# First modulation of a 14-stage kernel: shift and scale loaded before the gate, and x with its norm worked out beside the additions

## The chip, the cores and the metric

The kernel runs on one core of a Trainium2 chip. The metric is device time in microseconds (us) of one execution. Engines are called as in the profile: PE (TensorE, matrix products), DVE (VectorE), ACT (ScalarE), POOL (GpSimd) and SP (SyncE, which here only issues transfers). They run on their own instruction lists and meet at semaphores. SBUF is the on-chip memory of 128 partitions, PSUM the accumulation memory that PE writes.

## The reference, cut to what matters

Two networks follow each other (six sublayers, then eight). Each sublayer takes a 256 x 1024 activation `x`, normalizes it, scales and shifts it by vectors that come from a conditioning vector `c`, applies weights, and adds the result to `x` through a gate. The opening of the first sublayer is what this case is about:

```
c_act = silu(c)
mod = (c_act @ mod_w[layer] + mod_b[layer]).reshape(B, N_SUB, 3, D_MODEL)   # shift, scale, gate of each sublayer
h = rmsnorm(x, g) * (1 + scale) + shift
x = x + 0.5 * (1 + gate) * swiglu(h, w_gu, w_down)
```

`mod_w` has 3 x 1024 columns for each sublayer: 12.6 MB in float32 for the first sublayer. `lru_lambda` (used in the fifth stage) and the rotary positions (used from the seventh stage on) need small elementwise work that is also done in the opening. All arithmetic must stay in float32 quality.

## The kernel before, in words

Everything that streams from memory is float32. Weights come in chunks of 1 MB (`raw`, 4 buffers, issued by SP in `chunk`). A chunk is split in two pieces; ACT copies a piece to a high half (`w_hi`, function `pieces` in the ACT block), DVE subtracts to get the low half (`w_lo`, `pieces` in the DVE block), and PE multiplies three times (`a_hi*w_hi`, `a_lo*w_hi`, `a_hi*w_lo`). There are 4 buffers of pieces (`OPS`). A chunk's transfer waits until the low halves of the chunk four before it are made.

The modulation vectors of a sublayer are called a group. For a group, 16 units of 128 x 1536 of `mod_w` are loaded (`mod_raw`, two buffers, `h` = 0 or 1, issued by POOL in `mod_half`), and DVE adds each, times one entry of `silu(c)` per partition, to `mod_acc` (`mod_add`). PE then sums `mod_acc` over the partitions with 24 one-column products (`mod_sum`), and DVE finishes (`mod_finish`). Groups 1 to 13 are worked through during the stages before they are needed: in a "ffn1" stage one unit is added between every two pieces. POOL loads the next unit into a buffer when DVE has added the one before it (`mod_half` waits for `mod_used`). POOL also makes the low halves of the hidden activations (`hid_low`), one after each job.

A stage of kind "ffn1" starts with eleven jobs of 96 products each; a job needs four pieces. After a job ACT applies silu (`sig`), DVE multiplies (`product`, which frees the job's PSUM banks), ACT writes `hid_hi` and POOL `hid_lo`. A product waits until the low halves of two jobs before are made. In a job's DVE part the order is: two pieces, a unit with h = 0, two pieces, a unit with h = 1, the product. ACT makes the next-but-one job's first piece only behind `hid_hi` of a job.

Group 0 has nothing before it to hide behind. In the opening, SP issues the positions, `x`, 29 small vectors (all into `rows`), then 16 units of `first_mod` (7 buffers), then the weights. PE waits for all small vectors, transposes `x` and `rows`, DVE copies both out of PSUM, ACT makes silu(c) and two steps for lambda, DVE adds 16 units, then does the lambda series and the angles of the rotary positions, PE sums the 24 columns, DVE finishes group 0 and makes four low pieces, PE sums the squares of `x`, ACT takes the root, DVE inverts it and forms `tmp` and `a_lo` (`a_values`), and PE begins the first job. The order of all this is written out by hand, engine by engine; no scheduler moves it.

Of the kernel before, what the change touches and what calls it, by code (L numbers as in the profile page):

```python
# [15 lines left out]
P = 128  # L16
# [28 lines left out]
FIRSTS = 7  # L45
# [47 lines left out]
def build(nc, t, out, stop=None):  # L93
# [8 lines left out]
    with ctx:  # L102
# [43 lines left out]
        NLOADS = 1 + sum((ROW[n] + m - 1) // P - ROW[n] // P + 1 for n, m in vec)  # L146
# [83 lines left out]
        mod_used = sem("mod_used")  # L230
        turn_done = sem("turn_done")
# [180 lines left out]
        def mod_out(w):  # L412
            return bk[:, 4 * (w % 2) + 1, S:S + MODC // P]
# [39 lines left out]
        def _(sp):  # L453
# [18 lines left out]

            sp.dma_start(pos_i[:, :], t["positions_2"]).then_inc(pos_landed, 16)
            sp.dma_start(xin[:, :, :], t["x"][0].rearrange("(b p) d -> p b d", p=P)).then_inc(loaded, 16)
            for name, count in vec:
                src, r = vectors[name], 0
                while r < count:
                    a = ROW[name] + r
                    n = min(count - r, P - a % P)
                    sp.dma_start(rows[a % P:a % P + n, a // P, :], src[r:r + n, :]).then_inc(loaded, 16)  # L480
                    r += n
# [1582 lines left out]
```

## Time and profile before

| | us |
|---|---|
| median of 3 runs | 2570.82 |
| lowest, highest | 2563.72, 2575.38 |
| the profiled execution, its own time | 2580.46 |
| its span | 2578.8 |
| busy PE, DVE, ACT, POOL | 2358.3, 1666.9, 1199.6, 334.9 |

The span is the profiled stretch from the first to the last instruction; the profiled execution took 1.7 us more than its span, and 9.6 us more than the median of the runs. PE is busy for 91% of the span. In the first of 40 slices of the span (64.5 us each) PE's busy digit is 3 and the granted TensorE clock 0.6 of full speed; in the other slices PE's digit is 5 to 9. A row of the timeline gives start and length in us, the engine, the line of the kernel, the operation, what it writes and reads, and in brackets how long the engine had been idle and who ended that. Where a row has "x14" it stands for 14 instructions, and its length is from the start of the first to the end of the last.

### The profile page before, as it was taken

Reading aid. Unit: us, or ns where it says so; the run is one execution under the profiler, and the core shown is the slowest. Engines: PE = TensorE matmul, PEld = TensorE weight load, DVE = VectorE, ACT = ScalarE, POOL = GpSimd, SP = SyncE. Lnnn points to the kernel's source line nnn. Section 1 sums busy time; section 2 is a strip of 40 time slices with the busy share of each in tenths; the row PEclk is TensorE's granted clock in tenths of the full one; section 3 lists DMA queues with packets and bytes.
Section 4 is the critical chain, followed back from the end, with each engine's and each line's share of the span. In section 5 each row is a group of like instructions: output and inputs, shape, how many; then the busy total and the mean of one; then the engine's idle time right before and its main releaser. Section 6 shows DMA issues by size and latency. Waiting matters only on the chain.

```text
span 2578.8 us, 43638 instructions
## 1 busy us (share of the span) xinstructions
PE 2358.3 (91%) x17650; PEld 2262.1 (88%) x17650; DVE 1666.9 (65%) x1960; ACT 1199.6 (47%) x1761; POOL 334.9 (13%) x481
## 2 busy tenths in 40 slices
PE   3999999999999958999879999998997899888997
PEld 2999978999999957999848998888996899867997
DVE  6667655667767665767765766855766675654653
ACT  1444445543544464544534543435544554554543
POOL 0111000111111021211000214300201120000210
PEclk6999989999999988999869998998998999888999
DMA  8689763779688723878443775403784477222552
GB/s 309 233 283 315 254 233 102 269 269 326 241 299 293 251 82 124 307 263 296 158 164 104 250 272 183 131 3 121 253 275 133 139 255 249 82 98 66 181 191 70
DMA packets 292525, 523.88 MB, mean 203 GB/s; under 512 B 9318, under 2 KB 184849, under 8 KB 292369
## 3 DMA queue, kind: packets, MB, share of 16 engines
q1 hardware_dynamic: 262417, 358.07, 41.8%
q0 software_dynamic: 29952, 163.59, 17.8%
q8 instruction: 115, 1.88, 0.3%
q14 instruction: 41, 0.34, 0.0%
HBM read 520.57 MB, written 1.05 MB: 202 GB/s over the span
## 4 chain that ended last, share of the span: by engine, by line
PE 87%; DVE 7%; ACT 3%; issue 2%; POOL 0%; ACTq 0%; DVEq 0%; POOLq 0%
PE bk L1210 11%; PE bk L1211 11%; PE bk L1212 11%; PE bk L1118 10%; PE bk L1119 10%; PE bk L1120 10%; PE bk L1261 4%; PE bk L1171 3%; PE bk L1452 2%; PE bk L1191 1%; PE bk L1192 1%; PE bk L1193 1%; DVE inv L1623 1%; DVE mod_acc L1596 1%; PE bk L1316 1%
## 5 line engine op out<-in xcount | busy, mean ns | idle before, releaser
L1577 DVE TENSOR_TENSOR w_lo<-raw,w_hi 128x1024 fp32r<-128x1024 f32 (+5 forms) x720 | 834.2, 1185 | 611.2 <-ACT w_hi L721 609.2
L721 ACT ACTIVATE w_hi<-raw 128x1024 fp32r<-128x1024 f32 (+5 forms) x720 | 684.4, 977 | 737.2 <-PE bk L1120 402.8
L1210 PE MATMUL bk<-a_hi,w_hi 128*128 128x256 f32 x2336 | 668.5, 286 | 4.4 <-DVE a_lo L1643 4.4
L1211 PE MATMUL bk<-a_lo,w_hi 128*128 128x256 f32 x2336 | 667.1, 286 | 0.0
L1212 PE MATMUL bk<-a_hi,w_lo 128*128 128x256 f32 x2336 | 666.7, 285 | 0.0
L1118 PE MATMUL bk<-hid_hi,w_hi 128*128 128x256 f32 x1664 | 465.7, 280 | 0.0
L1120 PE MATMUL bk<-hid_hi,w_lo 128*128 128x256 f32 x1664 | 465.7, 280 | 0.0
L1119 PE MATMUL bk<-hid_lo,w_hi 128*128 128x256 f32 x1664 | 465.7, 280 | 0.0
L1210 PEld LDWEIGHTS bk<-a_hi,w_hi 128*128 128x128 f32 x2336 | 454.3, 194 | 5.1 <-issue 4.5
L1211 PEld LDWEIGHTS bk<-a_lo,w_hi 128*128 128x128 f32 x2336 | 454.2, 194 | 0.0
L1212 PEld LDWEIGHTS bk<-a_hi,w_lo 128*128 128x128 f32 x2336 | 453.9, 194 | 0.0
L1596 DVE SCALAR_TENSOR_TENSOR mod_acc<-mod_raw,cact,mod_acc 128x1536 f32<-128x1536 f32 x182 | 329.8, 1812 | 10.8 <-DMA mod_raw<-in_ada_w 6.3
L1118 PEld LDWEIGHTS bk<-hid_hi,w_hi 128*128 128x128 f32 x1664 | 313.0, 188 | 0.0
L1119 PEld LDWEIGHTS bk<-hid_lo,w_hi 128*128 128x128 f32 x1664 | 313.0, 188 | 0.0
L1120 PEld LDWEIGHTS bk<-hid_hi,w_lo 128*128 128x128 f32 x1664 | 312.9, 188 | 0.0
L600 POOL TENSOR_TENSOR hid_lo<-ev,hid_hi 128x512 f32 (+1 forms) x108 | 138.6, 1296 | 821.6 <-ACT hid_hi L849 685.8
L1118 PE MATMUL bk<-a_hi,w_hi 128*128 128x256 f32 x576 | 167.5, 291 | 36.6 <-POOL a_lo L700 29.4
L1119 PE MATMUL bk<-a_lo,w_hi 128*128 128x256 f32 x576 | 166.5, 289 | 0.0
L1120 PE MATMUL bk<-a_hi,w_lo 128*128 128x256 f32 x576 | 166.3, 289 | 0.0
L563 POOL DMA_DIRECT2D mod_raw<-in_ada_w x128 | 69.2, 541 | 671.1 <-DVE mod_acc L1596 529.6
L1118 PEld LDWEIGHTS bk<-a_hi,w_hi 128*128 128x128 f32 x576 | 114.3, 199 | 38.2 <-issue 34.5
L1261 PEld LDWEIGHTS bk<-one,mod_acc 128*128 128x128 f32 x672 | 100.5, 241 | 31.4 <-issue 28.9
(327 smaller groups left out, 3174.8 us busy)
## 6 DMA issues: line engine op xcount, KB each, us to landing
raw<-in_ffn_w SPq DMA_DIRECT2D x128, 1024.0 KB, 5.5
mod_raw<-in_ada_w POOLq DMA_DIRECT2D x128, 768.0 KB, 6.0
raw<-in_ffn_w_gu SPq DMA_DIRECT2D x88, 1024.0 KB, 7.1
mod_raw<-in_mod_w POOLq DMA_DIRECT2D x80, 768.0 KB, 6.7
raw<-in_ffn_w_down SPq DMA_DIRECT2D x40, 1024.0 KB, 6.7
first_mod<-in_mod_w SPq DMA_DIRECT2D x16, 768.0 KB, 6.2
raw<-in_sb_w_qkv SPq DMA_DIRECT2D x12, 1024.0 KB, 5.2
raw<-in_conv_w_pw SPq DMA_DIRECT2D x12, 1024.0 KB, 5.5
```

The costliest lines, as they stand in the source:

```text
L600: pool.tensor_tensor(hid_lo[:, tiles(pair, width), :], ev[:, slot, :, :], hid_hi[:, tiles(pair, width), :].bitcast(F32), ALU.subtract).the ...
L721: ins = act.activation(o(w_hi[:, p % OPS, :]), r(raw[:, c % RAWS, :]), ACT.Copy)
L1118: pe.matmul(o, wh[:, s], xh, start=first, stop=False)
L1119: pe.matmul(o, wh[:, s], xl, start=False, stop=False)
L1120: ins = pe.matmul(o, wl[:, s], xh, start=False, stop=last)
L1171: ins = pe.matmul(job_flat(w, S), ones[:, :], sq_of(j), start=(j == 0), stop=(j == KD - 1))
L1210: pe.matmul(o, wh, a_hi[:, f, :], start=(f == 0), stop=False)
L1211: pe.matmul(o, wh, a_lo[:, f, :], start=False, stop=False)
L1212: ins = pe.matmul(o, wl, a_hi[:, f, :], start=False, stop=(f == KD - 1))
L1261: ins = pe.matmul(mod_out(w)[:, j:j + 1], mod_acc[:, P * j:P * j + P], one1[:, 0:1], start=True, stop=True)
L1577: ins = dve.tensor_tensor(o(w_lo[:, p % OPS, :]), r(raw[:, c % RAWS, :]), o(w_hi[:, p % OPS, :].bitcast(F32)), ALU.subtract)
L1596: dve.scalar_tensor_tensor(out=a, in0=src, scalar=cc[:, bass.ds(r, 1)], in1=a, op0=ALU.mult, op1=ALU.add).then_inc(mod_used, 1)
```

## The change

Group 0 is taken apart. Shift and scale (columns 0 to 2047) are loaded as 16 units of 128 x 1024 instead of 128 x 1536, first the eight of the shift, then the eight of the scale, into 10 buffers. The gate's 8 units (128 x 1024) are loaded by SP after the first four weight chunks, once all 16 additions are done, and are multiplied and added by POOL (8 multiplications, 7 additions, `gate_acc`) during the first jobs, between its unit loads for group 1. PE sums the gate's columns (`gate_sum`) beside the sum of group 1 in job 8, and DVE finishes it there.

`c` has its own two small transfers (`crow`) at the head of SP's list and its own transposition; the small vectors are issued by ACT instead of SP; `x` is issued after two units and copied out of PSUM by ACT; the squares of `x` are summed before the modulation sums. Low pieces 0 to 3 are made before group 0 is finished, and the lambda series and the angles are made after `a_values` of the first stage. The sine of the angles is taken at the end of the first stage's jobs.

The core of the diff:

```diff
-FIRSTS = 7
+FIRSTS = 10
@@ SP
+            for h, name in enumerate(("c", "c_2")):
+                sp.dma_start(crow[h * KD:h * KD + KD, :], as_rows(t[name])).then_inc(c_landed, 16)
             sp.dma_start(pos_i[:, :], t["positions_2"]).then_inc(pos_landed, 16)
-            sp.dma_start(xin[:, :, :], t["x"][0].rearrange("(b p) d -> p b d", p=P)).then_inc(loaded, 16)
-            for name, count in vec:
...
             for u in range(UNITS):
+                if u == 2:
+                    sp.dma_start(xin[:, :, :], t["x"][0].rearrange("(b p) d -> p b d", p=P)).then_inc(x_landed, 16)
                 if u >= FIRSTS:
                     sp.wait_ge(mod_used, 2 + u - FIRSTS + 1)
                 w, at = mod_of(0)
-                sp.dma_start(first_mod[:, u % FIRSTS, :], w[u // 2 * P:u // 2 * P + P, at + u % 2 * MODW:at + (u % 2 + 1) * MODW])\
+                sp.dma_start(first_mod[:, u % FIRSTS, :], w[u % KD * P:u % KD * P + P, at + u // KD * D:at + (u // KD + 1) * D])\
                     .then_inc(first_landed[u % FIRSTS], 16)
+            def first_gates():
+                sp.wait_ge(mod_used, 2 + UNITS)
+                sp.wait_ge(x_turned, 1)
+                sp.wait_ge(turn_read, 1)
+                w, at = mod_of(0)
+                for j in range(KD):
+                    sp.dma_start(gate_raw[j // 4][:, j % 4, :], w[j * P:j * P + P, at + 2 * D:at + 3 * D]).then_inc(gate_landed[j], 16)
...
+                    if st["n"] == 0:
+                        for b in range(4):
+                            narrow(c + b, wg, b // 2 * 256 + b % 2 * F1)
+                        first_gates()
@@ POOL
-                    mod_rest(g, lambda i, b: hid_low(n + 2 * i + b, 2 * i + b, b))
+                    if st["n"] == 0:
+                        for j in range(KD):
+                            pool.wait_ge(gate_landed[j], 16)
+                            src = gate_raw[j // 4][:, j % 4, :]
+                            if j == 0:
+                                pool.tensor_scalar(gate_acc[:, :], src, cact[:, 0:1], None, ALU.mult).then_inc(gate_made, 1)
+                            else:
+                                pool.wait_ge(gate_made, 2 * j - 1)
+                                pool.tensor_scalar(src, src, cact[:, j:j + 1], None, ALU.mult).then_inc(gate_made, 1)
+                                pool.wait_ge(gate_made, 2 * j)
+                                pool.tensor_tensor(gate_acc[:, :], gate_acc[:, :], src, ALU.add).then_inc(gate_made, 1)
+                            if j % 2:
+                                mod_half(g, j // 4 + 1, j // 2 % 2)
+                            if j == 3:
+                                hid_low(n, 0, 0)
+                        hid_low(n + 1, 1, 1)
...
@@ ACT
+                    act.dma_start(rows[a % P:a % P + n, a // P, :], src[r:r + n, :]).then_inc(loaded, 16)
...
+                    if at == 8:
+                        act.wait_ge(consts, 1)
+                        act.wait_ge(c_turned, 1)
+                        act.activation(cact[:, :], bk[:, 7, 0:2 * KD], ACT.Silu).then_inc(cact_ready, 1)
+            act.wait_ge(x_turned, 1)
+            for h in range(2):
+                act.activation(x[:, 4 * h:4 * h + 4, :].rearrange("p k s -> p (k s)"), job_flat(0, 2048)[:, 1024 * h:1024 * h + 1024],
+                               ACT.Copy).then_inc(x_in, 1)
@@ PE
-            mod_sum(0, 1)
+            pe.wait_ge(x_in, 2)
+            sums(0, 0, KD)
             turned()
+            for h in range(2):
+                pe.wait_ge(mod_used, 2 + KD * (h + 1))
+                for j in range(KD * h, KD * h + KD):
+                    ins = pe.matmul(mod_out(1)[:, j:j + 1], mod_acc[:, P * j:P * j + P], one1[:, 0:1], start=True, stop=True)
...
+            def gate_sum(w):
+                pe.wait_ge(gate_made, 2 * KD - 1)
+                for j in range(KD):
+                    pe.matmul(mod_out(w, MODC // P + KD)[:, MODC // P + j:MODC // P + j + 1], gate_acc[:, P * j:P * j + P], one1[:, 0:1],
+                              start=True, stop=True)
```

DVE in the opening, before: `first_mod` are the 16 units, `cols` the turned small vectors, `lsp` the lambda series (its first row), `rs` the angles (their last row), `w_lo` the four low pieces, `tmp` the first of `a_values`.

```order
L1601 COPY x<-bk 128x2048
L1601 COPY cols<-bk 128x938
L1594 TENSOR_SCALAR mod_acc<-first_mod,cact 128x1536 x2
L1596 SCALAR_TENSOR_TENSOR mod_acc<-first_mod,cact,mod_acc 128x1536 x14
L1701 TENSOR_SCALAR lsp<-lsp 128x10
...
L1732 TENSOR_SCALAR rs<-rs 32x256
L1606 TENSOR_TENSOR mv<-bk,cols 128x24
L1609 SCALAR_TENSOR_TENSOR mv_a<-mv,cols 128x8
L1617 TENSOR_SCALAR mv_g<-mv 128x8
L1577 TENSOR_TENSOR w_lo<-raw,w_hi 128x1024 x4
L1623 RECIPROCAL inv<-rms 128x256
L1638 SCALAR_TENSOR_TENSOR tmp<-x,mv_a,inv 128x256 x3
```

The same place now:

```order
L1681 TENSOR_SCALAR mod_acc<-first_mod,cact 128x1024
L1683 SCALAR_TENSOR_TENSOR mod_acc<-first_mod,cact,mod_acc 128x1024 x7
L1688 COPY cols<-bk 128x922
...
L1681 TENSOR_SCALAR mod_acc<-first_mod,cact 128x1024
L1683 SCALAR_TENSOR_TENSOR mod_acc<-first_mod,cact,mod_acc 128x1024 x7
L1662 TENSOR_TENSOR w_lo<-raw,w_hi 128x1024 x4
L1828 TENSOR_TENSOR mv<-bk,cols 128x16
L1830 SCALAR_TENSOR_TENSOR mv_a<-mv,cols 128x8
L1710 RECIPROCAL inv<-rms 128x256
L1725 SCALAR_TENSOR_TENSOR tmp<-x,mv_a,inv 128x256 x3
```

The copy of `x` is gone from DVE, the units are shorter, the small vectors come out between the two sets of eight, and the lambda series and the angles (35 instructions) stand behind `a_values`, ahead of low piece 4.

POOL in the first stage, before: from the first two unit loads of group 1 to the low half of the first job.

```order
L563 DMA mod_raw<-in_mod_w 128x1536 x2
...
L563 DMA mod_raw<-in_mod_w 128x1536
L562 REGISTER_ALU
L563 ISA
L563 DMA mod_raw<-in_mod_w 128x1536
L600 ISA x2
L600 TENSOR_TENSOR hid_lo<-ev,hid_hi 128x512
```

The same place now (the number behind `gate_raw` tells its two halves apart):

```order
L584 DMA mod_raw<-in_mod_w 128x1536 x2
L703 TENSOR_SCALAR gate_acc<-gate_raw_62,cact 128x1024
L706 TENSOR_SCALAR gate_raw_62<-gate_raw_62,cact 128x1024
L708 TENSOR_TENSOR gate_acc<-gate_acc,gate_raw_62 128x1024
L584 DMA mod_raw<-in_mod_w 128x1536
L706 TENSOR_SCALAR gate_raw_62<-gate_raw_62,cact 128x1024
L708 TENSOR_TENSOR gate_acc<-gate_acc,gate_raw_62 128x1024
L706 TENSOR_SCALAR gate_raw_62<-gate_raw_62,cact 128x1024
L708 TENSOR_TENSOR gate_acc<-gate_acc,gate_raw_62 128x1024
L584 DMA mod_raw<-in_mod_w 128x1536
L621 TENSOR_TENSOR hid_lo<-ev,hid_hi 128x512
```

Two unit loads of group 1 stood directly behind each other; now four gate instructions stand between one load and the next, here and twice more behind these rows.

## Rows read from the trace of the kernel before

**Rows 1.** Page: busy time by engine.

```profile
PE 2358.3 (91%) x17650; PEld 2262.1 (88%) x17650; DVE 1666.9 (65%) x1960; ACT 1199.6 (47%) x1761; POOL 334.9 (13%) x481
```

**Rows 2.** Timeline of PE, 0 to 150 us.

```profile
17.98 1.96 PE L1251 MATMUL bk<-ident,rows 128*128 128x128 f32 x8
...
51.27 10.37 PE L1261 MATMUL bk<-one,mod_acc 128*128 128x1 f32 x48 [28.51 <-DVE mod_acc L1596]
61.92 3.78 PE L1171 MATMUL bk<-sig,ones 128*128 128x256 f32 x8 [0.28 <-DVE mv L1606]
...
72.82 0.55 PE L1191 MATMUL bk<-a_hi,w_hi 128*128 128x256 f32 x1 [4.15 <-DVE a_lo L1643]
```

**Rows 3.** Timeline of DVE, 0 to 78 us.

```profile
20.43 1.13 DVE L1601 COPY cols<-bk 128x938 f32<-128x938 f32 x1
...
26.83 24.29 DVE L1596 SCALAR_TENSOR_TENSOR mod_acc<-first_mod,cact,mod_acc 128x1536 f32<-128x1536 f32 x14
...
60.31 0.28 DVE L1732 TENSOR_SCALAR rs<-rs 32x256 f32<-32x256 f32 x1
...
62.05 4.62 DVE L1577 TENSOR_TENSOR w_lo<-raw,w_hi 128x1024 fp32r<-128x1024 f32 x4
69.21 1.75 DVE L1623 RECIPROCAL inv<-rms 128x256 f32<-128x256 f32 x1 [2.54 <-ACT rms L746]
71.00 1.28 DVE L1638 SCALAR_TENSOR_TENSOR tmp<-x,mv_a,inv 128x256 f32<-128x256 f32 x3
...
76.15 1.27 DVE L1643 SCALAR_TENSOR_TENSOR a_lo<-tmp,mv,a_hi 128x256 fp32r<-128x256 f32 x3
```

**Rows 4.** Timeline of SP's DMA issues, from the start.

```profile
1.36 0.41 SPq L474 DMA_DIRECT2D xin<-in_x  x1
...
12.44 26.93 SPq L486 DMA_DIRECT2D first_mod<-in_mod_w  x16
```

**Rows 5.** Windows (start:end, length, busy times, clock, DMA share, GB/s).

```profile
30.00:40.00 10.00, 0.00 (x0) 0.00 (x0) 10.00 (x7) 0.00 (x0) 0.00 (x0) 0.50 1.01 411
...
72.00:78.30 6.30, 5.48 (x26) 5.51 (x27) 5.42 (x14) 3.42 (x8) 0.00 (x0) 0.50 0.02 7
78.30:84.00 5.70, 5.70 (x49) 5.70 (x49) 0.28 (x1) 2.34 (x2) 0.00 (x0) 1.00 0.00 0
...
150.00:173.30 23.30, 23.30 (x197) 23.30 (x196) 18.14 (x15) 12.92 (x15) 5.31 (x7) 1.00 0.95 327
```

**Rows 6.** Timeline of DVE in the first jobs.

```profile
89.26 1.01 DVE L1594 TENSOR_SCALAR mod_acc<-mod_raw,cact 128x1536 f32<-128x1536 f32 x1
...
104.31 0.67 DVE L1943 TENSOR_TENSOR ev<-sig,bk 128x512 f32<-128x512 f32 x1
108.16 2.36 DVE L1577 TENSOR_TENSOR w_lo<-raw,w_hi 128x1024 fp32r<-128x1024 f32 x2 [3.18 <-ACT w_hi L721]
...
116.17 0.68 DVE L1943 TENSOR_TENSOR ev<-sig,bk 128x512 f32<-128x512 f32 x1
118.60 2.82 DVE L1577 TENSOR_TENSOR w_lo<-raw,w_hi 128x1024 fp32r<-128x1024 f32 x2 [1.75 <-ACT w_hi L721]
```

**Rows 7.** POOL: timeline of a load, then groups by form, then line 664.

```profile
90.97 0.54 POOL L563 DMA_DIRECT2D mod_raw<-in_mod_w  x1 [38.98 <-DVE mod_acc L1594]
...
L600 POOL TENSOR_TENSOR hid_lo<-ev,hid_hi 128x512 f32 x88 | 112.8, 1297 | 695.4 <-ACT hid_hi L849 685.8 <-ACT hid_hi L1001 9.6
...
L685 POOL MEMSET sb_m<- 128x384 f32 x1 | 0.4, 418 | 1.5 <-PE bk L1156 1.5
...
L664 POOL TENSOR_SCALAR diag<-ident,cols x62: 595/606/2620, 1586.2 to 1632.8; 128x128 f32<-128x128 f32 x62
```

**Rows 8.** Timeline of DVE while POOL makes the diagonals.

```profile
1610.98 1.82 DVE L1643 SCALAR_TENSOR_TENSOR a_lo<-tmp,mv,a_hi 128x256 fp32r<-128x256 f32 x3
```

**Rows 9.** DMA issues, 0 to 110 us: size, us to landing.

```profile
mod_raw<-in_mod_w POOLq DMA_DIRECT2D x6, 768.0 KB, 7.5
```

**Rows 10.** Chain of waits, 0 to 200 us: the sum of group 1.

```profile
173.39 6.37 PE bk L1261 x48
```

More of the change, by code:

```diff
@@ L145, in build @@
             assert vectors[name].shape[0] == count, (name, vectors[name].shape, count)
-        NLOADS = 1 + sum((ROW[n] + m - 1) // P - ROW[n] // P + 1 for n, m in vec)
+        NLOADS = sum((ROW[n] + m - 1) // P - ROW[n] // P + 1 for n, m in vec)
         NPT = -(-NROW // P)
@@ L230, in build @@
         mod_used = sem("mod_used")
+        gate_landed = [sem(f"gate_landed{i}") for i in range(KD)]
+        gate_made = sem("gate_made")
+        c_landed = sem("c_landed")
+        c_turned = sem("c_turned")
+        x_landed = sem("x_landed")
+        x_turned = sem("x_turned")
+        x_in = sem("x_in")
         turn_done = sem("turn_done")
@@ L1012, in _ @@
                         gated(w + b, b % 2, b)
+                    if g == 0:
+                        act.wait_ge(rope_arg, 1)
+                        act.activation(rope[NOPE:P, :], rs[NOPE:P, 0, :], ACT.Sin).then_inc(rope_ready, 1)
                     pieces(p + 48, p + 61)
@@ L1291, in _ @@
                     mod_sum(st["late"], w + 1)
-                if after(g) != "plain":
+                if after(g) not in ("plain", "first"):
                     sums(w, 0, KD)
@@ L1690, in _ @@
             dve.tensor_copy(pos_f[:, :], pos_i[:, :]).then_inc(pos_ready, 1)
-            turn_in(x[:, :, :].rearrange("p k s -> p (k s)"), 0, 2048)
+            dve.wait_ge(cact_ready, 1)
+            for r in range(KD):
+                mod_add(0, r, 0)
             turn_in(cols[:, 0:NROW], 1, NROW)
-            dve.wait_ge(turn_read, 2)
-            dve.wait_ge(cact_ready, 2)
+            dve.wait_ge(rope_in, 1)
+            own_wait(own(dve.tensor_copy(rcol[:, :], bk[:, 6, 0:2])))
+            dve.tensor_scalar(rs[:, 0, :], bk[:, 6, S:2 * S], rcol[:, 0:1], None, ALU.mult).then_inc(rope_read, 1)
@@ L1695, in _ @@
             for r in range(KD):
-                for h in range(2):
-                    mod_add(0, r, h)
-            u, r, r2, s = (lsp[:, j, :] for j in (1, 2, 3, 0))
-            own_wait(own(dve.tensor_scalar(r, u, 2.0, None, ALU.add)))
-            own_wait(own(dve.reciprocal(r2, r)))
-            own_wait(own(dve.tensor_tensor(r, u, r2, ALU.mult)))
-            own_wait(own(dve.tensor_tensor(r2, r, r, ALU.mult)))
-            own_wait(own(dve.tensor_scalar(s, r2, 1.0 / 17, 1.0 / 15, ALU.mult, ALU.add)))
@@ L1738, in _ @@
+            pieces(0, 4)
+            first_finish()
             for st in stages:
@@ L1741, in _ @@
                     final_norm()
-                elif after(g) == "first":
-                    pieces(p + 2, p + 4)
                 elif after(g) == "post":
```

166 lines of the change are left out of this document (105 added, 61 removed).

## The prediction

> **What bounds the kernel now.** I read the page first: PE is busy for 91% of the span [rows 1], so once the first job runs, time that PE doesn't lose is fixed. Then the timeline of PE: it stands idle for 28.5 us for DVE's additions, and the first real product begins at 72.82 us [rows 2]. Let T0 be that moment. Ahead of it there is one chain. The timeline of DVE and of the issues show it: the units are issued only from 12.44 us on, behind the small vectors [rows 4]; DVE adds 14 of the 16 in 24.29 us, 1.735 each [rows 3], while the transfers run at 411 GB/s with all DMA engines busy [rows 5]; then come 24 column sums in 10.37 us, the sums of squares in 6.8 (two rows), the inverse and `a_values` [rows 2, 3]. Behind T0 the window 150 to 173.3 shows PE busy without a gap and DVE busy for 18.1 of 23.3 us [rows 5]: DVE has some 2.6 us to spare per job, no more. A job is 96 products; 197 records in 23.3 us make 11.4 us of it, after a first one with 26 products at half clock until 78.3 (0.5, that is 1.2 GHz) [rows 5]. So job 1 begins at T0+13.9, job 3 at T0+36.6, job 4 at T0+48. In the timeline of DVE the product of job 1 ends at 104.98 and the piece that job 3 begins with is ready at 109.3, T0+36.5 [rows 6]: PE is fed with no margin there. What makes DVE late in the first jobs makes PE late by nearly as much.
>
> **The opening: where T0 goes.** c and the positions come first, at 0.41 us an issue [rows 4], so unit 0 is issued at some 2.1 us instead of 12.44. Until the last unit 8.4 MB of units, 1.05 MB of x and 0.5 MB of small vectors pass: 9.9 MB at 411 GB/s are 24 us, so it lands at about 28. DVE needs 1.735 x 1024/1536 = 1.16 us for a unit, 9.1 for eight. The small vectors are now 27 issues on ACT, some 0.4 each, with silu between: the last at about 12. Before, PE waited until 14.5 for them; now they share the DMA engines with the units, for which landing takes up to 7.5 us [rows 9]: I take 17 (bounds 14.5 and 22). PE's 1.96 for turning them [rows 2], the copy's 1.13 [rows 3] and the angles' first two steps behind PE's small products end at 22. The second eight end at 31.1, after the DMA bound of 29. They were over at 51.1 [rows 3].
>
> Behind them only eight column sums remain, at 10.37/24 = 0.43 us each 3.5 us, and they lie beside DVE's low pieces. The sums of squares (6.8) lie beside the second eight. What is late next are the four low pieces: chunks 0 and 1 (2.1 MB) land at 33 to 34, ACT needs 2 us for the last two high halves, DVE 1.2 for the last low: 37.2. Group 0's end takes 0.4, and from the inverse to T0 it is 72.82 - 69.21 = 3.6 us [rows 2, 3]. T0 is 41.2, 31.6 us earlier; between 38 (everything lands early) and 46 (small vectors at 22).
>
> **The moved elementwise work.** Lambda and angles ran from 51.1 to 60.6 [rows 3], less 0.7 for what stays in the opening: 8.8 us. They now start where `a_values` ends, 77.4 or T0+4.6, and end at T0+13.4; low piece 4 is ready at T0+14.6 where PE wants it at T0+13.9. 0 to 3 us; I take 1.
>
> **The gate on POOL.** This is the term that decides. POOL's order puts four gate instructions between two unit loads of group 1, three times, and its first such load waits until DVE has added the unit before, 89.26 + 1.01, the load following at 90.97 or T0+18.2 [rows 6, 7]. Units 0 to 1 of the gate (3 instructions) are done before, then POOL waits; with the 1 us above it goes on at T0+19. From there to the load of the second half of unit pair 2: 6 multiplications, 6 additions, one `hid_low`, three issues.
>
> An addition of 128 x 1024 is not in the trace; 128 x 512 took 1.297 [rows 7], so at most 2.6, and 2.5 is taken. A multiplication of 128 x 128 took 0.606 [rows 7]. If all of it were paid per element, 128 x 1024 costs 4.85; if it grows as the memset does (418 ns for 384 elements, 1.09 ns each), 0.61 + 896 x 1.09 = 1.6. I take 1.6: while POOL made those products DVE's three `a_lo` took 1.82 instead of 1.27 [rows 8, 3], 0.18 more each, so an instruction of 0.606 kept DVE off for a third of its time, and the rest looks fixed.
>
> The same two rows show that POOL and DVE hold each other up. The Trainium skill (SBUF - State Buffer, "Who interferes with whom") has the reason: a DVE instruction with two SBUF inputs and a GpSimd instruction that reads SBUF exclude each other, and the second waits for the whole of the first. The trace agrees, 1.82 against 1.27. By that rule nothing of the gate is free beside the low pieces.
>
> 6 x 1.6 + 6 x 2.5 + 1.3 + 3 x 0.54 + some 16 handovers of 0.1 are 29.1 us. For the waits on DVE's own instructions I add 4: the 12 instructions each meet at most one of 1.2 us, so 0 to 14, but DVE itself stands waiting for a unit for about half of the stretch. The load is issued at T0+52.1; landing took 7.5 with full queues [rows 9], and they are emptier here: 6. DVE adds (1.8), multiplies (0.68), and the first piece of job 4 is ready 3.2 us later (116.85 to 120.0) [rows 6]: T0+63.8, against T0+48. PE loses 15.8 us, of it about 6 already ahead of job 3, because the load in the middle is late in the same way. After that POOL has no gate work and the old rhythm returns; the lost time doesn't.
>
> The Trainium skill (GPSIMD Engine Reference, "Engine selection") calls one-input work on GpSimd roughly line rate; an estimate from its 1.03 cycles an element at 1.2 GHz is 0.9 us for 1024 elements plus the fixed part, 1.4 in all. No row here has such a size. The sum would be 1.2 us lower by it.
>
> **Clock and gate sum.** Ahead of job 4 PE is idle for about 7 us. After 4.15 us of idleness its first 26 products ran at 0.5 [rows 2, 5], 0.213 instead of 0.118 us each: 2.4 us, if the clock falls (0 to 4.8, with two falls). The gate adds 8 column sums in job 8: 16 records at 6.37/48 [rows 10], 2.1 us, on PE.
>
> **Sum.** 31.6 - 15.8 - 2.4 - 2.1 = 11.3; the 1 us is in the 19. The profiled execution took 2580.46, so it would be 2569; the median of the runs is 9.6 lower: 2559.
>
> **Rivals.** (a) POOL's work is hidden after all: DVE's spare time and the low traffic let the units be in time. For it speaks DVE's 22% idle time in rows 5, against it that POOL's waits are fixed in its order. Then 31.6 - 1 - 2.1 = 28 are gained: 2543. Part of it (the waits on DVE near 0, landing 4.5, no fall of the clock) gives 19: 2552. (b) Slower than before: POOL's multiplication costs 4.85. Six of them add 19.5 us, and the twelve instructions meet DVE's with the full 14: 31.6 - 15.8 - 19.5 - 10 - 4.5 = -18, 2589. It decides from about 4 us a multiplication on. Rows 8 speak against it. (c) Between: waits of 8 to 10 and two falls of the clock give a gain of 3: 2568. (d) The small vectors land late on ACT's queue, at 22, T0 at 46: a gain of 6, 2565. (e) The opening doesn't shorten, because T0 waits for the weights, which are loaded last: they need 12 MB at 411 GB/s, 29 us, so this cannot hold T0 beyond 46; the change does what it says unless a wait that I missed stands there: 2571.
>
> **How the numbers follow.** Forecast (gain 7 to 17) 0.38, (a) with its part 0.26, (c) 0.18, (d) 0.06, (b) 0.08, (e) 0.04. Half a per cent is 12.9 us, about what a measurement can tell from no change, and the forecast lies just inside it: half of its chance is on either side. Faster by over 0.5%: 0.19 + 0.26 = 0.45. Within: 0.19 + 0.18 + 0.06 + 0.02 = 0.45. Slower: 0.10. The range reaches over (a) on one side, and on the other over (c), (d) and (e): 2543 to 2577.
>
> **What would show it.** First product at 38 to 46 us. The gate's multiplication near 1.6 and addition near 2.5 us on POOL. DVE waiting for a unit of group 1 (`mod_add` after a DMA) three times between T0+30 and T0+60, the longest last; PE idle ahead of jobs 3 and 4, together 10 to 20 us; granted clock 0.5 at the head of job 4. Wrong if PE runs through the first five jobs without a gap (then (a)), if T0 is beyond 46, or if a multiplication takes over 3 us.

## The result and the profile after

The changed kernel is slower: 2587.07 us (2576.58 to 2594.01, 7 runs) against 2574.18 (2563.72 to 2578.07, 7 runs), ratio 1.0053 with a 95% interval of 1.0036 to 1.0071, that is 13 us. The prediction, 2559 with 2543 to 2577, was wrong in sign and in range. Its base was the median of the first three runs before, 2570.82; with seven it is 2574.18.

The two profiled executions hide this: the span after is 2575.0 us at a mean granted clock of 0.936, before 2578.8 at 0.927. The one of after was the fastest of its runs. Whole spans of two executions are therefore not compared below. What is compared is the first sublayer, which ends for PE with the first product of the next sums of squares (`bk<-ev,ones`): at 274.75 us before, at 285.32 after, 10.6 later. The row of before:

```profile
274.75 0.70 PE L1171 MATMUL bk<-ev,ones 128*128 128x256 f32 x2 [1.15 <-ACT ev L734]
```

The page of the changed kernel, busy times, beside [rows 1]:

```profile
PE 2349.6 (91%) x17651; PEld 2256.4 (88%) x17651; DVE 1663.6 (65%) x1960; ACT 1200.6 (47%) x1761; POOL 387.6 (15%) x496
```

Timeline of PE in the changed kernel (start, length, operation, idle time before it and who ended it), beside [rows 2]:

```profile
30.81 1.99 PE L1310 MATMUL bk<-ident,rows 128*128 128x128 f32 x8 [16.22 <-DMA rows<-in_pool_scale]
...
45.83 3.58 PE L1352 MATMUL bk<-one,mod_acc 128*128 128x1 f32 x16 [3.04 <-DVE mod_acc L1683]
...
54.22 0.55 PE L1250 MATMUL bk<-a_hi,w_hi 128*128 128x256 f32 x1 [4.81 <-DVE a_lo L1730]
71.92 0.55 PE L1269 MATMUL bk<-a_hi,w_hi 128*128 128x256 f32 x1 [4.59 <-DVE w_lo L1662]
100.75 0.39 PE L1269 MATMUL bk<-a_hi,w_hi 128*128 128x256 f32 x1 [2.98 <-DVE w_lo L1662]
112.75 0.58 PE L1269 MATMUL bk<-a_hi,w_hi 128*128 128x256 f32 x1 [4.50 <-DVE w_lo L1662]
128.18 0.58 PE L1269 MATMUL bk<-a_hi,w_hi 128*128 128x256 f32 x1 [6.78 <-DVE w_lo L1662]
...
285.32 0.70 PE L1230 MATMUL bk<-ev,ones 128*128 128x256 f32 x2 [1.14 <-ACT ev L777]
```

The first product comes at 54.22 instead of 72.82, so the opening did get shorter, by 18.6 us. It waits for the small vectors, which PE turns at 30.81 (17.98 before). From there on PE is idle four times, 18.85 us in all: ahead of job 1, ahead of job 3, in the middle of job 3 and ahead of job 4 (96 products are a job, so these places follow from counting). Before, the same stretch had no wait over 0.1 us. The last row says where it ends: the sublayer behind T0 (the first product of the first job) takes 231.1 us instead of 201.9, so 29.2 are lost and 18.6 gained.

ACT's issues and the transfer behind them, from the chain of waits of the changed kernel (0 to 200 us: start, length, what):

```profile
9.59 3.20 ACTq L853
12.81 1.32 ACTq L853
...
15.59 15.18 DMA rows<-in_pool_scale
```

The last of the 27 transfers is issued at 15.59, and all of them are in only 15.2 us later, though the last is 4 KB.

Windows of the changed kernel (start:end, length, then busy time and instructions of PE, PEld, DVE, ACT and POOL, granted clock, DMA share, GB/s), from 6 to 86 us behind T0:

```profile
60.00:80.00 20.00, 15.41 (x108) 15.23 (x107) 17.31 (x44) 8.61 (x9) 6.81 (x4) 0.83 0.68 224
80.00:100.00 20.00, 17.77 (x149) 17.57 (x147) 12.94 (x8) 7.34 (x9) 19.45 (x8) 1.00 0.59 197
100.00:120.00 20.00, 14.75 (x86) 14.55 (x87) 7.23 (x5) 4.16 (x5) 19.50 (x10) 0.74 0.46 152
120.00:140.00 20.00, 13.22 (x95) 13.01 (x94) 12.57 (x11) 9.14 (x11) 4.35 (x6) 0.83 0.78 269
```

POOL is busy for 19.45 and 19.50 of 20 us in the middle two, where DVE is busy for 12.94 and 7.23 and the DMA engines for half of the time: DVE waits for data that POOL has not asked for. The granted clock is 0.83, 0.74 and 0.83 in the rows with a long wait; the 438 products of the four rows take 61.2 us of busy time.

Timeline of POOL in the changed kernel, its first gate row, then from the load of the first half of unit pair 1 (74.14) to that of the second half of pair 2 (117.73):

```profile
51.50 2.85 POOL L703 TENSOR_SCALAR gate_acc<-gate_raw,cact 128x1024 f32<-128x1024 f32 x1 [4.87 <-DMA gate_raw<-in_mod_w]
...
74.14 0.60 POOL L584 DMA_DIRECT2D mod_raw<-in_mod_w  x1 [13.06 <-DVE mod_acc L1681]
74.79 3.96 POOL L706 TENSOR_SCALAR gate_raw<-gate_raw,cact 128x1024 f32<-128x1024 f32 x1
78.83 2.42 POOL L708 TENSOR_TENSOR gate_acc<-gate_acc,gate_raw 128x1024 f32<-128x1024 f32 x1
...
107.60 2.35 POOL L708 TENSOR_TENSOR gate_acc<-gate_acc,gate_raw 128x1024 f32<-128x1024 f32 x1
110.12 5.20 POOL L706 TENSOR_SCALAR gate_raw<-gate_raw,cact 128x1024 f32<-128x1024 f32 x1 [0.18 <-POOL gate_acc L708]
115.41 2.37 POOL L708 TENSOR_TENSOR gate_acc<-gate_acc,gate_raw 128x1024 f32<-128x1024 f32 x1
117.73 0.60 POOL L584 DMA_DIRECT2D mod_raw<-in_mod_w  x1
```

and DVE at the other end of it, same kernel:

```profile
85.89 1.21 DVE L1662 TENSOR_TENSOR w_lo<-raw,w_hi 128x1024 fp32r<-128x1024 f32 x1
87.39 3.06 DVE L1662 TENSOR_TENSOR w_lo<-raw,w_hi 128x1024 fp32r<-128x1024 f32 x1 [0.28 <-ACT w_hi L764]
93.88 1.82 DVE L1683 SCALAR_TENSOR_TENSOR mod_acc<-mod_raw,cact,mod_acc 128x1536 f32<-128x1536 f32 x1 [3.42 <-DMA mod_raw<-in_mod_w]
...
109.28 2.29 DVE L1683 SCALAR_TENSOR_TENSOR mod_acc<-mod_raw,cact,mod_acc 128x1536 f32<-128x1536 f32 x1 [7.45 <-DMA mod_raw<-in_mod_w]
...
122.50 1.82 DVE L1683 SCALAR_TENSOR_TENSOR mod_acc<-mod_raw,cact,mod_acc 128x1536 f32<-128x1536 f32 x1 [7.82 <-DMA mod_raw<-in_mod_w]
```

Three waits for a unit, the longest last, at T0+40, +55 and +68: the mechanism that the prediction described, larger and later (it had T0+30 to T0+60). A multiplication left alone takes 2.84 us (2.84 and 2.85 occur four times), the longest 5.20; an addition alone 2.35, the longest 3.44. The subtraction of DVE is 1.21 or 3.06.

### The profile page after: what moved, and what is told of

Read it like the earlier page. It is cut to its first block, busy times and chain, and to the rows that moved or that the text cites. A ratio compares the mean times of both kernels' runs of the same rounds, so it can differ in the third digit from the quotient of the medians.

```text
span 2575.0 us, 43605 instructions
## 1 busy us (share of the span) xinstructions
PE 2349.6 (91%) x17651; PEld 2256.4 (88%) x17651; DVE 1663.6 (65%) x1960; ACT 1200.6 (47%) x1761; POOL 387.6 (15%) x496
## 4 chain that ended last, share of the span: by engine, by line
PE 84%; DVE 7%; ACT 3%; issue 2%; POOL 2%; DMA 1%; ACTq 1%; DVEq 0%; SPq 0%; POOLq 0%
PE bk L1269 11%; PE bk L1270 11%; PE bk L1271 11%; PE bk L1177 10%; PE bk L1179 10%; PE bk L1178 10%; PE bk L1320 3%; PE bk L1230 3%; PE bk L1531 2%; PE bk L1250 1%; PE bk L1251 1%; DVE mod_acc L1683 1%; PE bk L1252 1%; POOL gate_raw L706 1%; DVE inv L1710 1%
## 5 line engine op out<-in xcount | busy, mean ns | idle before, releaser
L1270 PEld LDWEIGHTS bk<-a_lo,w_hi 128*128 128x128 f32 x2336 | 457.5, 196 | 0.0
L1178 PEld LDWEIGHTS bk<-a_lo,w_hi 128*128 128x128 f32 x576 | 114.8, 199 | 0.0
```

The lines of the kernel that those rows point to most:

```text
L1178: pe.matmul(o, wh[:, s], xl, start=False, stop=False)
L1270: pe.matmul(o, wh, a_lo[:, f, :], start=False, stop=False)
```

## The experiments

There were two theories at first. A: the changed kernel loses by two things, the small vectors that land late and the first gate's work on POOL, which delays the unit loads. B: the waits come from the landing of gate and units, or from the lambda series and the angles in their new place, and POOL's work is only beside them. In the table T0 is the first real product, "end" the end of the first sublayer for PE against 274.75 before, both from the profile; the time is the median, the ratio against the kernel before on the same chip. "Vectors" and "loads" are the second and third experiments' edits.

| kernel | T0 | end | median us | ratio |
|---|---|---|---|---|
| changed | 54.22 | +10.6 | 2587.07 | 1.0053 [1.0036, 1.0071] |
| one gate row | 54.17 | -16.0 | 2560.11 | 0.9942 [0.9923, 0.9962] |
| vectors on SP | 46.03 | +5.2 | 2581.86 | 1.0026 [1.0008, 1.0043] |
| loads on SP | 53.86 | +2.8 | 2581.08 | 1.0021 [0.9996, 1.0047] |
| vectors, loads | 46.56 | -2.0 | 2572.12 | 0.9981 [0.9964, 0.9999] |
| the same, POOL starts late | 46.64 | -3.6 | 2574.77 | 1.0015 [0.9997, 1.0033] |
| the same, multiplied by ACT | 46.49 | -7.6 | 2571.35 | 1.0000 [0.9983, 1.0017] |
| the same, both | 46.57 | -6.9 | 2569.95 | 0.9990 [0.9971, 1.0009] |
| one row, vectors | 46.33 | -19.7 | 2555.63 | 0.9935 [0.9914, 0.9956] |
| gate on DVE | 54.11 | -14.0 | 2561.11 | 0.9947 [0.9928, 0.9966] |
| gate on DVE, vectors | 46.14 | -21.9 | 2551.16 | 0.9920 [0.9897, 0.9942] |
| the same, series cut | 46.18 | -20.5 | 2559.95 | 0.9931 [0.9908, 0.9955] |
| gate on DVE, SP holds | 48.36 | -19.5 | 2556.91 | 0.9937 [0.9910, 0.9964] |

The difference of the medians and "end" agree within 7 us in every row. Behind the first sublayer the program does the same work, but its time differs from one execution to the next: 2289.7 us after at a mean clock of 0.936, 2304.0 before at 0.927 (span less end).

**One gate row.** In the loop over the rows of the first gate:

```
-   pool.tensor_scalar(src, src, cact[:, j:j + 1], None, ALU.mult).then_inc(gate_made, 1)
-   pool.wait_ge(gate_made, 2 * j)
-   pool.tensor_tensor(gate_acc[:, :], gate_acc[:, :], src, ALU.add).then_inc(gate_made, 1)
+   pool.sem_inc(gate_made, 2)
```

> The changed kernel, but POOL multiplies only the first of the gate's eight rows and adds none; all transfers stay. It leaves out 7 of 8 rows of the first gate. Theory A (POOL's gate instructions hold back the unit loads of group 1, and DVE and PE wait for them): first product still at 54 us, job 4 begins near 106 instead of 128.2, the time falls by about 22 us against the changed kernel, to 2565. Rival B (the gate's 4.2 MB crowd the weights' and units' transfers, or the clock is what costs): job 4 stays beyond 120, time 2580 to 2587.

Its T0 is that of the changed kernel and its transfers too; what it leaves out is POOL's arithmetic on seven of the eight rows. Timeline of PE, all waits from T0 to the end of the sublayer:

```profile
54.17 0.55 PE L1248 MATMUL bk<-a_hi,w_hi 128*128 128x256 f32 x1 [4.71 <-DVE a_lo L1728]
68.95 0.36 PE L1267 MATMUL bk<-a_hi,w_hi 128*128 128x256 f32 x1 [1.16 <-DVE w_lo L1660]
258.74 0.70 PE L1228 MATMUL bk<-ev,ones 128*128 128x256 f32 x2 [1.14 <-ACT ev L775]
```

One wait of 1.16 us stays, that of the lambda series and the angles; the sublayer ends 26.6 us earlier. In 60 to 140 us it runs 664 products where the changed kernel runs 438: 17.7 us of the 26.6 are PE's idle time (61.15 against 78.84 busy). The other 8.9 are products at the lower clock: from T0 to the end the same 1650 records take 211.1 us of busy time in the changed kernel and 202.3 here. A holds, B falls: POOL's gate work costs 26.6 us, and what the clock costs is part of that, since the falls behind the waits are gone with them.

**Small vectors on SP's queue.** The 27 issues go from ACT to SP, behind unit 7:

```
 for u in range(UNITS):
+    if u == KD:  # the loop over vec, word for word from ACT
+        sp.dma_start(rows[a % P:a % P + n, a // P, :], src[r:r + n, :]).then_inc(loaded, 16)
```

> The changed kernel with the 27 small vectors issued by SP behind unit 7 instead of by ACT. Theory A (the small transfers of ACT's queue trickle through beside SP's large ones, so they landed at 30.8 us): in the order of one queue they land near 18.5 to 20, the second eight units are bound by the transfers, first product at 43 to 45 instead of 54.2, time 10 us lower than the changed kernel, 2577. Rival B (small rows are slow beside large ones on any queue): they land at 28 or later, first product at 52 or later, time 2585 or more.

PE's timeline:

```profile
22.73 1.99 PE L1308 MATMUL bk<-ident,rows 128*128 128x128 f32 x8 [9.06 <-DMA rows<-in_pool_scale]
46.03 0.55 PE L1248 MATMUL bk<-a_hi,w_hi 128*128 128x256 f32 x1 [4.71 <-DVE a_lo L1728]
```

The vectors are in 8.1 us earlier and T0 comes 8.2 earlier, so they set T0 one to one. It is 1 us beyond A's range, and the time, 2581.86, lies between A's 2577 and B's 2585, because the end moves only 5.4: PE waits 5.66, 3.24, 4.50 and 6.92 us at the old four places, 1.5 more in all. The gate's rows land only 2.2 us earlier, POOL starts at 49.27, T0+3.2 instead of T0-2.7, and so holds more of DVE's work ahead of job 1. The other 1.3 are the clock: PE's 1650 records take 212.4 us of busy time instead of 211.1.

**Three unit loads on SP's queue.** SP issues the halves of units 1 to 3 of group 1 between the weights, POOL keeps the gate:

```
+    sp.wait_ge(mod_used, UNITS + 2 * r + h + 1)
+    sp.dma_start(mod_raw[:, h, :], w[...]).then_inc(sp_landed[h], 16)   # one behind each chunk, from the seventh on
-    if j % 2: mod_half(g, j // 4 + 1, j // 2 % 2)                       # POOL
```

> The changed kernel with the unit loads 1 to 3 of group 1 issued by SP between its weight chunks instead of by POOL between gate instructions. Theory A (place in POOL's order): first product at 54, no wait for a unit before 130 us, job 4 begins at 110 to 114 instead of 128.2; what is left is the moved elementwise work (3.8) and about 4 us of POOL and DVE excluding each other; time 15 to 18 us lower than the changed kernel, about 2570. Rival B (exclusion between POOL's and DVE's instructions is the main part): DVE's low pieces stay late, job 4 at 120 or later, time lower by 5 at most.

The waits for units went, and a new one came: PE idle 10.91 us at 77.98, ahead of job 1. The median is 6 us lower, not A's 15 to 18, and job 4 begins at 117.13, between A's 110 to 114 and B's 120: neither theory holds as written. Both edits together:

> Both edits together: small vectors by SP behind unit 7, unit loads 1 to 3 by SP. If the two losses add: first product at 43 to 45, job 4 at 100 to 104, time about 27 us lower than the changed kernel, 2559 to 2562, and 12 to 15 below the kernel before. Rival: with the first product earlier, POOL's chain (8 multiplications of 2.85 and 7 additions of 2.4, 40 us from the gate's landing) becomes the bound for the product of job 3, which waits for the second low half: then only 18 to 20 us lower, 2568.

The sublayer ended 12.5 us earlier than in the changed kernel, not 27, and the time is 4 us above what the rival said. PE is idle 12.30 us at 73.31. DVE's timeline there shows why:

```profile
54.16 1.04 DVE L1812 TENSOR_SCALAR lsp<-lsp 128x10 f32<-128x10 f32 x1
55.23 0.17 DVE L1811 TENSOR_TENSOR lsp<-lsp 128x10 f32<-128x10 f32 x1
...
57.17 2.26 DVE L1812 TENSOR_SCALAR lsp<-lsp 128x10 f32<-128x10 f32 x1
...
68.05 2.39 DVE L1829 TENSOR_SCALAR rs<-rs 128x256 f32<-128x256 f32 x1
```

and POOL's:

```profile
54.06 2.85 POOL L725 TENSOR_SCALAR gate_raw<-gate_raw,cact 128x1024 f32<-128x1024 f32 x1 [0.17 <-POOL gate_acc L722]
56.99 2.42 POOL L727 TENSOR_TENSOR gate_acc<-gate_acc,gate_raw 128x1024 f32<-128x1024 f32 x1
...
67.95 2.34 POOL L727 TENSOR_TENSOR gate_acc<-gate_acc,gate_raw 128x1024 f32<-128x1024 f32 x1
```

An instruction of 10 elements a row, 0.17 us elsewhere in this series, takes 2.26 while POOL adds at 56.99, and one of 0.29 takes 2.39 while POOL adds at 67.95. Series and angles take 20.9 us (51.08 to 71.94); in the changed kernel, where POOL stood still from 61.08 to 74.14, they took 8.9 (61.67 to 70.55). Theory A had missed this: POOL's gate costs even when it delays no load. The Trainium skill (SBUF - State Buffer, "Who interferes with whom") describes it as an exclusive lock held for a whole instruction. For the addition the trace agrees: the DVE instruction from 57.17 ends at 59.43, the addition at 59.41. For the multiplication it does not: beside the one from 54.06 to 56.91 DVE waits in the instruction of 1.04 us, then runs five of 0.17 from 55.23 on, while POOL is still at work, and is held again only near its end (0.68 from 56.26).

**POOL starts when the angles are made**, on top of these two edits:

```
+   pool.wait_ge(rope_arg, 1)     # ahead of the first row of the gate
```

> The kernel with the small vectors on SP's queue and three unit loads on SP's queue (2572.1 us), and POOL now begins with the gate's eight multiplications and seven additions only when DVE has made the angles. Theory A (POOL's gate work stretches the series for lambda and the angles, which took 20.9 us from 51.08 there and 8.9 us after 61.67 in the changed kernel, where POOL stood still): the stretch from the series to the angles takes 9 us again and ends at 60, the idle time of PE ahead of job 1 (12.3 us) falls to 1 or 2, jobs 1 to 3 lose 2 to 4 us more than before because the same POOL work now stands beside them: 2562 to 2566 us. Rival B (the time is only moved: DVE's subtractions and additions of jobs 1 to 3 are held as long as the series was): 2569 to 2573 us, with PE idle 8 us or more in jobs 1 to 4.

PE idle 1.19 us ahead of job 1, as A said, but 3.96 at 88.73 and 7.93 at 122.83, the end only 1.7 us earlier, and the ratio no better; the median, 2574.77, is even above the rival's 2573. The rival is right in the mechanism: two subtractions of DVE take 4.55 us in three places beside POOL (2.36 alone). Part of the last wait is order and not the memory port: DVE stands 3.91 us ahead of a product, at 117.69, for a `hid_lo` that POOL makes only behind its gate rows. Moved in time, POOL's 39 us (8 x 2.84 + 7 x 2.35) were paid at another place.

**The multiplications on ACT**, without and with the late start of POOL's additions:

```
+   act.wait_ge(gate_landed[j], 16)
+   act.activation(src, src, ACT.Copy, scale=cact[:, j:j + 1]).then_inc(gate_mul, 1)   # behind a_high, eight times
```

> The kernel with vectors and three unit loads on SP's queue (2572.1 us), and the eight multiplications of the first gate made by ACT behind its rounding of a; POOL keeps seven additions, which then stand back to back. In the trace of that kernel single DVE instructions of the series are held 2.3 us while POOL adds (57.17 2.26, 68.05 2.39) and about 1 us while POOL multiplies (54.16 1.04). Theory A (the additions hold DVE most): the series still ends late, at 68 to 73, PE is idle 8 to 13 us ahead of job 1, but POOL is through at 75 instead of 110, and jobs 2 to 4 wait for nothing: 2566 to 2571 us. Rival B (what counts is the sum of POOL's time beside the series, which halves): PE idle 4 to 6 us ahead of job 1, 2560 to 2564 us.

> Both: the multiplications on ACT, and POOL's seven additions only when the angles are made. Theory A: series and angles 9 us, PE idle 1 to 2 us ahead of job 1, the additions from 61 to 79 cost 1 to 3 us in job 1 and 2, nothing later: 2558 to 2563 us, the fastest of the complete kernels and 11 to 16 us below the kernel before. Rival B (ACT's eight multiplications hold up its rounding of the weights of job 1): PE idle 4 us or more ahead of job 1 for w_hi, 2564 to 2568 us.

Without the late start: PE idle 8.16 us ahead of job 1 and 3.60 at 97.33, the end 5.6 earlier, 2571.35, at the edge of A; that jobs 2 to 4 would wait for nothing did not hold. With it the rival's wait came, and the time is 2 us above its range. ACT's and DVE's timeline:

```profile
52.91 7.56 ACT L902 ACTIVATE gate_raw<-gate_raw,cact 128x1024 f32<-128x1024 f32 x6 [0.29 <-DMA gate_raw<-in_mod_w]
60.49 1.28 ACT L782 ACT_TABLE_LOAD   x1
61.78 3.90 ACT L782 ACTIVATE w_hi<-raw 128x1024 fp32r<-128x1024 f32 x4
```

```profile
62.87 6.47 DVE L1675 TENSOR_TENSOR w_lo<-raw,w_hi 128x1024 fp32r<-128x1024 f32 x2 [2.93 <-ACT w_hi L782]
```

ACT multiplies until 60.5, its rounding of the first piece of job 1 starts at 61.78 instead of 56.66 (in the kernel without these multiplications), and then DVE's two subtractions meet POOL's additions: 6.47 us for 2.36. PE is idle 5.75 us ahead of job 1.

**One row and the vectors on SP's queue:**

> POOL makes one row of the first gate only (seven of the eight rows of that gate are left out), and the small vectors come on SP's queue. One row alone gave 2560.1 us with the first product at 54.2; the vectors alone moved the first product to 46.0. If the start of the chain passes on whole when POOL's work is out of the way (theory A): first product at 46, 2551 to 2554 us, 20 to 23 us below the kernel before. Rival B (another limit stands behind it, such as the landings of job 1's weights or the clock): 2556 us or more, with a wait on PE for a landing in jobs 0 to 2.

2555.63 and T0 46.33: 8 us earlier at T0 and only 4 of them in the time, between the theories' figures; the profile shows no new wait but the 1.67 us ahead of job 1, and the end is at 255.10, 3.6 earlier than with one row alone. From T0 to the end it takes 4.2 us more: 0.5 is that wait, and 3.7 is busy time of the same 1650 records (205.96 against 202.26). Of these 3.2 lie in job 8, beside the column sums: the granted clock is 0.50 there from 151 to 164 us, and with one row alone only from 161 to 167.5. Whether the edit has a part in that isn't shown; the next pair, where T0 moves by as much, loses nothing.

**The gate on DVE.** DVE makes one multiply-and-add per row, two behind the product of each of the first four jobs; POOL only loads and makes `hid_lo`:

```
+   dve.wait_ge(gate_landed[j], 16)
+   dve.wait_ge(gate_made, j)
+   dve.scalar_tensor_tensor(out=gate_acc[:, :], in0=src, scalar=cact[:, j:j + 1], in1=gate_acc[:, :],
+                            op0=ALU.mult, op1=ALU.add).then_inc(gate_made, 1)
```

> The changed kernel (2587 us) with one alteration: the first gate is made by DVE instead of POOL, with one multiply-and-add per row of 128x1024, two of them behind the product of each of the first four jobs; POOL only issues the unit loads and makes the low halves of hid. Theory A (the changed kernel loses by POOL's gate work: its unit loads come late and its multiplications and additions hold DVE's instructions): eight DVE instructions of about 1.2 us stand where DVE waits 1.8 to 3.2 us per job for ACT's rounding, POOL loads each unit at once, no wait on PE above 2 us in jobs 1 to 8: 2560 to 2565 us, close to the kernel with one gate row (2560.1). Rival B (DVE has no room in these jobs; 10 us more of its work show on PE): PE waits of 1 to 3 us in each of four jobs, 2567 to 2572 us.

> The gate on DVE as before, and the small vectors on SP's queue behind unit 7, so that the first product comes at 46 instead of 54. The same pair with one gate row left gave 2555.6 us. Theory A: 2554 to 2560 us, 4 to 6 below the kernel with the gate on DVE alone and 13 to 18 below the kernel before. Rival B (the gate's rows, issued by SP behind the unit loads, land after DVE wants them, as they land at 50 to 58): a wait on gate_raw in job 0 or 1 and 2560 to 2565 us.

DVE and POOL in job 2, gate alone moved, and then PE with the vectors on SP's queue too:

```profile
86.30 3.51 DVE L2043 SCALAR_TENSOR_TENSOR gate_acc<-gate_raw,cact,gate_acc 128x1024 f32<-128x1024 f32 x2
...
87.23 1.49 POOL L621 TENSOR_TENSOR hid_lo<-ev,hid_hi 128x512 fp32r<-128x512 f32 x1 [0.63 <-ACT hid_hi L1042]
...
89.73 2.35 DVE L1647 TENSOR_TENSOR w_lo<-raw,w_hi 128x1024 fp32r<-128x1024 f32 x2
```

```profile
46.14 0.55 PE L1233 MATMUL bk<-a_hi,w_hi 128*128 128x256 f32 x1 [4.71 <-DVE a_lo L1713]
60.92 0.36 PE L1252 MATMUL bk<-a_hi,w_hi 128*128 128x256 f32 x1 [1.54 <-DVE w_lo L1645]
252.86 0.70 PE L1213 MATMUL bk<-ev,ones 128*128 128x256 f32 x2 [1.15 <-ACT ev L770]
```

PE has one wait over 0.2 us left between T0 and the end. With the gate on DVE the time is 2561.11, as theory A said and as with one row; 26 us below the changed kernel with nothing left out. With the vectors on SP's queue T0 comes 8.0 us earlier and the end 7.9, and the time is 2551.16, the fastest and 3 us below A's range: below the kernel before by 0.8% (0.6 to 1.0), 15 to 27 us. No wait for a gate row shows on DVE or PE, so rival B falls. That is the version to keep.

**The series cut in two**, angles behind the first low half of job 1:

> The kernel with the gate on DVE and the vectors on SP's queue, with the series for lambda and the angles cut in two: the series stays behind the values of a, the angles go behind the low half of the first piece of job 1. Theory A (the 9 us of the two stand ahead of that low half and leave PE idle 1.2 to 1.7 us ahead of job 1): that wait goes, 1 to 2 us faster than without the cut. Rival B (the angles then delay the next low halves just as much): the wait moves to another piece of job 1 and the time stays within 1 us.

```profile
56.80 1.23 DVE L1645 TENSOR_TENSOR w_lo<-raw,w_hi 128x1024 fp32r<-128x1024 f32 x1 [1.29 <-ACT w_hi L757]
```

The wait of 1.54 us ahead of job 1 shrinks to 0.43, and job 1 begins 1.1 us earlier. But jobs 1 to 4 then take 12.5, 12.0, 12.0 and 12.0 us instead of 11.6, 11.5, 11.5 and 11.5, and the end comes 1.4 us later. The row shows why: DVE now reaches the first piece of job 1 before ACT has rounded it and stands 1.29 us, time that the angles filled before. Without the cut DVE was busy for 39.68 us of the 40 from 60 to 100 us, so it had no room to catch up. That is the rival's mechanism, and 0.4 us more than its 1 us. The median is 8.8 higher, with intervals that overlap for the most part; how much of that is this 1.4 and how much the spread of executions stays open.

**SP holds unit 8 back** until the small vectors are in, with the vectors on ACT's queue:

```
+   if u == KD:
+       sp.wait_ge(loaded, 16 * NLOADS)
```

> The kernel with the gate on DVE (2561.1 us, small vectors on ACT's queue, first product at 54.1), and SP issues unit 8 and all behind it only when the 27 small vectors have landed. In the changed kernel ACT issued them from 1.11 to 15.9 us and they were used from 30.81 on; put on SP's queue they were issued from 6.6 to 18.9 and used from 22.84 on. Theory A (they are slow because the DMA engines serve the full queue of SP beside them): once units 0 to 7 and x are in, at about 16, nothing stands against them, PE turns them at 17 to 20, the first product comes at 45 to 49 although the units 8 to 15 start later, and the time is 2553 to 2559 us. Rival B (these small transfers take as long by themselves on this queue): they are turned at 25 or later, the first product comes at 54 or later, 2561 us or more.

```profile
22.12 1.99 PE L1297 MATMUL bk<-ident,rows 128*128 128x128 f32 x8 [7.75 <-DMA rows<-in_pool_scale]
```

ACT's last issue was at 15.42, as in the changed kernel (15.59), and the vectors were turned at 22.12 instead of 30.81, T0 was 48.36 instead of 54.11. So SP's transfers from unit 8 on, beside them, cost 8.7 of the 15 us; A holds, in T0 and time too, though the vectors came 2 us later than it said. From 20 to 22 us 34 packets were left on ACT's queue and the DMA engines were busy for 0.02 of the time: these last transfers were slow with nothing beside them.

## Why the prediction was wrong, step by step

The prediction made a gain of 11.3 us in the profiled execution; the sublayer lost 10.6. Of the 21.9 between them 13.0 are T0 and 8.9 what stands behind it. The medians lie 28 us above the forecast: besides these 21.9, 3.4 are the median of before, which seven runs raised, and 2.8 lie behind the sublayer, unassigned.

- **"I take 17 (bounds 14.5 and 22)" for the small vectors: failed.** They were used from 30.81, outside the bounds. The bound of 22 came from 7.5 us of landing for one unit [rows 9]; that the engines serve 27 small transfers of a second queue beside a full one had no row before. T0 was 54.22, not 41.2. With the vectors at 22.73 it was 46.03: the rest of the chain was sized right to within some 1 us (41.2 + 5.7 = 46.9).
- **"0 to 3 us; I take 1" for lambda and angles: right alone, wrong beside POOL.** 1.16 with one gate row, 1.38 with the gate on DVE; 4.59 in the changed kernel, where POOL's second multiplication stretched a `tmp` (1.25 us instead of 0.47) and its first addition, 58.38 to 61.08, the last `a_lo` (three in 3.42 us instead of 1.27), just ahead of the series.
- **"I take 1.6" for POOL's multiplication: failed, and the term that decided behind T0.** It is 2.84 alone. From the load at 74.14 to that at 117.73 the prediction had 33.1 us; it was 43.6. Six multiplications took 22.4 instead of 9.6 us, six additions 16.8 instead of 15, together 10.5 more than the sum with its 4 us of waits. By the lengths alone (2.84 and 2.35) 7.4 of this are the multiplication and 4 the waits on DVE's instructions, which came to 8 instead of 4; the additions give back 0.9. The reason given, that most of 0.606 us is fixed [rows 7, 8], was wrong: a straight line through 0.606 for 128 and 2.84 for 1024 elements gives 2.5 ns an element, and 0.29 us fixed. The range had both ends, 1.6 and 4.85; I took the one of a memset, an operation that reads nothing. By the Trainium skill (GPSIMD Engine Reference, "Engine selection": roughly line rate; "Elementwise — side-by-side cycle accounting": 1.03 cycles an element) the estimate was 1.4, half of the measured 2.84; the measurement decides.
- **The addition, 2.5: right** (2.35 alone), from 1.297 for half the size [rows 7].
- **PE's lag, 15.8 us: too small.** Job 4 starts at 128.18, T0+74.0, instead of T0+63.8; against T0+48 that is a lag of 26.
- **Clock, 2.4: failed.** One fall was taken, at most two; the granted clock was 0.50 four times, once behind each wait (72.0 to 77.7, 102 to 105, 113 to 118.5 and 128.2 to 132.3 us). The products from T0 on took 8.8 us more than with one gate row, most of it inside the lag of 26.
- **Gate sum, 2.1: right** (1.84 for the 16 records).
- **The chances.** The rival (b) named the right side and mechanism, POOL's multiplication, but "it decides from about 4 us a multiplication on" assumed T0 at 41.2. With T0 13 us later 2.84, 3.7 beside DVE, were enough. Rival (d), late vectors, was bounded at 22. Both rivals came true together, and no case had them together. With the error in T0 alone the gain would have been 11.3 - 13.0 = -1.7, about 2573; with the 8.9 behind it alone 2.4, about 2568. Either lies inside the range, both together (-10.6) do not.
- **The signs.** Two of the signs of being wrong were met or nearly so: T0 beyond 46 (54.2), and a multiplication of over 3 us (2.84 alone, 3.7 beside DVE). The signs of the mechanism were met too: three waits for a unit with the longest last, PE idle 14.3 us ahead of and in job 3 and ahead of job 4, clock 0.50 at the head of job 4.

Settled are the two causes and their prices in this sublayer: POOL's gate work 26.6 us, the vectors' late landing 8 us at T0, of which 5.4 reached the end of the sublayer while POOL kept the gate and 7.9 with the gate on DVE. Open is how the 8.7 us of the vectors' landing divide between bandwidth and order on the DMA engines, and how much of POOL's 26.6 us in the changed kernel is the late loads and how much the held DVE instructions: taking the loads away gave 7 to 8, but lengthened the other part.

## What to carry to other kernels

Work moved to an engine that also issues loads must be priced as more than its own time: the delay of those loads and of what else stands behind it in that engine's list, and the time for which it holds the neighbour's instructions. Moving the loads away from it, moving it in time and giving half of it to ACT gave back 7 to 13 us of 26.6 here, with the vectors on SP's queue in each (ends +5.2 against -2.0, -3.6, -7.6 and -6.9); putting it as half as many instructions onto the engine that waited gave back 24.5 (+10.6 against -14.0). Small transfers that the start waits for need a place in the queue, not a queue of their own: on ACT's queue from 1.1 us on they were later than on SP's from 6.6 us on. And when several unknown costs delay the same chain, one case must have them all at their bad end.

## What the runs showed of the hardware

- Shares of a second queue. In the changed kernel SP's queue (q1) and ACT's (q10), DMA packets, MB and share of the engines, first 5 to 10, then 20 to 25 us, when ACT had issued all:

```profile
q1 hardware_dynamic: 508, 1.90, 97.8%
q10 hardware_dynamic: 176, 0.06, 5.0%
...
q1 hardware_dynamic: 532, 1.94, 100.1%
q10 hardware_dynamic: 66, 0.03, 2.2%
```

  The Trainium skill (DMA: Bandwidth & Descriptors, "Queues, rings and completion order") says that an engine takes packets from its queues in turn; summed over the 16 engines this trace shows 176 to 508 and then 66 to 532, not equal numbers, with transfers of q10 still on the way. Which engines held work of q10 no view shows, so the rule for one engine is not tested by that. ACT's own issue also stood for 3.20 and 1.32 us at two of the 27.
- POOL multiplies 128x1024 by a column in 2.84 us and adds 128x1024 in 2.35. DVE does both in one instruction, 1.28 us alone; the pair at 86.30 took 3.51, because its second, 2.13, stood beside POOL's `hid_lo` (87.23 to 88.72).
- DVE's instructions beside POOL's additions: 0.17 became 2.26, 0.29 became 2.39, 1.21 became 3.06, and two subtractions of 2.36 became 6.47 us; POOL's multiplication went from 2.84 to 5.20. Three additions back to back (52.71 to 60.30, multiplied by ACT) let DVE finish two instructions of the series each, in 2.27 and 0.17, 2.34 and 0.17, 2.33 and 0.17. Beside POOL's multiplication of 2.85 DVE lost some 1.4 us, in two pieces (1.04 and 0.68 for instructions of 0.17).
